# Two heads side by side in the array: scores and values of one attention, rotary scores of another

## The reference

```python
# first block: 8 heads of 64; with 256 tokens each query sees its own block only, causally
q = _rope(_rms_norm(q, q_norm_g[l]), pos)
k = _rope(_rms_norm(k, k_norm_g[l]), pos)
s_own = jnp.einsum('hqd,hjd->hqj', q_c, k_own, ...) * scale
s_own = jnp.where((k_pos[None, :] <= q_pos[:, None])[None], s_own, -jnp.inf)
p = jax.nn.softmax(scores, axis=-1)          # then p @ v, by head

# second block: 6 heads, keys of 128 (own) + 64 (rotary, shared by all heads), values of 128
q = jnp.concatenate([q_nope, q_rope], axis=-1)
k = jnp.concatenate([k_nope, k_rope], axis=-1)      # 256 tokens and 256 of the context: 512 keys
s = jnp.einsum('bqhd,bkhd->bhqk', q_blk, k, ...) * scale
pr = jax.nn.softmax(s, axis=-1)
return jnp.einsum('bhqk,bkhd->bqhd', pr, v)
```

## Time and profile before

| what | value |
|---|---|
| median of 3 runs | 1614.91 us (1614.48 to 1618.3) |
| the profiled execution, its own time | 1612.96 us |
| its span, first to last instruction | 1611.1 us |
| TensorE busy | 1546.0 us (96%) |
| VectorE busy | 407.1 us (25%) |
| ScalarE busy | 301.7 us (19%) |
| DMA, mean | 319 GB/s; from about 685 us on some 428 GB/s in nearly all slices |
| mean granted TensorE clock | 0.996 |

### The profile page before, as it was taken

The page is one execution under the profiler, slowest core; times in us unless marked ns, Lnnn a source line. Parts: engine busy times, 40 slices in busy tenths (PEclk is TensorE's granted clock), DMA queues, the critical chain, the costliest instruction groups (busy, mean ns, idle before and its releaser), DMA issues.

```text
span 1611.1 us, 18676 instructions
## 1 busy us (share of the span) xinstructions
PE 1546.0 (96%) x7234; PEld 851.3 (53%) x7234; DVE 407.1 (25%) x865; ACT 301.7 (19%) x618; POOL 9.1 (1%) x19
## 2 busy tenths in 40 slices
PE   9999999999999999999999999899999999998997
PEld 8666767888888756533333333324433333332332
DVE  1564244222223224431212121111112121111112
ACT  2223131111112234310111011111101110110111
POOL 0000000000000000000000000000000000000000
PEclk9999999999999999999999999999999999999999
DMA  9623675744443120699999999999989999999996
GB/s 389 247 105 128 283 320 190 280 157 157 150 144 123 53 105 24 280 428 428 423 428 428 429 429 428 429 428 427 418 362 426 430 429 428 428 429 428 428 428 272
DMA packets 44897, 513.34 MB, mean 319 GB/s; under 512 B 5120, under 2 KB 5264, under 8 KB 7088
## 3 DMA queue, kind: packets, MB, share of 16 engines
q1 hardware_dynamic: 43632, 507.69, 76.2%
q0 software_dynamic: 1216, 4.96, 0.9%
HBM read 511.58 MB, written 1.06 MB: 318 GB/s over the span
## 4 chain that ended last, share of the span: by engine, by line
PE 74%; DMA 20%; DVE 3%; ACT 2%; issue 1%; DVEq 0%; ACTq 0%; SPq 0%
PE bank L1165 26%; PE bank L615 12%; DMA ring<-in_gate_w 9%; PE bank L864 9%; DMA ring<-in_up_w 8%; PE bank L873 5%; DMA ring<-in_down_w 3%; PE bank L1257 3%; PE bank L1137 2%; PE bank L1197 2%; PE bank L1032 2%; PE bank L724 2%; PE bank L1182 1%; PE bank L653 1%; PE bank L680 1%; DVE squares L1865 1%
## 5 line engine op out<-in xcount | busy, mean ns | idle before, releaser
L1165 PE MATMUL bank<-ring,probs_slab 128*64 128x512 f32 x2928 | 660.6, 598 | 33.3 <-DMA ring<-in_gate_w 12.7
L1165 PEld LDWEIGHTS bank<-ring,probs_slab 128*64 128x64 f32 x2928 | 200.7, 137 | 424.4 <-issue 380.8
L864 PE MATMUL bank<-normed,ring 128*128 128x256 f32 x704 | 153.7, 379 | 0.0
L864 PEld LDWEIGHTS bank<-normed,ring 128*128 128x128 f32 x704 | 133.7, 190 | 19.0 <-issue 0.8
L2210 DVE TENSOR_TENSOR normed<-bank,big_slab 128x512 f32<-128x512 f32 x31 | 21.4, 692 | 430.7 <-PE bank L1182 430.7
L615 PE MATMUL bank<-normed,ring 128*128 128x256 f32 x448 | 98.5, 380 | 0.8 <-ACT normed L1393 0.8
L615 PEld LDWEIGHTS bank<-normed,ring 128*128 128x128 f32 x448 | 84.2, 190 | 15.1 <-issue 2.8
L2000 DVE SCALAR_TENSOR_TENSOR big_slab<-bank,par,big_slab 128x255 f32<-128x255 f32 x88 | 42.4, 482 | 166.3 <-ACT big_slab L1527 158.7
L873 PE MATMUL bank<-big_slab,ring 128*128 128x256 f32 x352 | 77.6, 379 | 0.0
L873 PEld LDWEIGHTS bank<-big_slab,ring 128*128 128x128 f32 x352 | 66.9, 190 | 9.1
L1197 PE MATMUL bank<-squares,mixed_slab 64*128 64x512 f32 x248 | 61.6, 615 | 6.3 <-ACT squares L1678 6.3
(11 more groups left out here) (332 smaller groups left out, 1179.7 us busy)
## 6 DMA issues: line engine op xcount, KB each, us to landing
ring<-in_up_w SPq DMA_DIRECT2D x63, 2048.0 KB, 22.1
ring<-in_down_w SPq DMA_DIRECT2D x63, 2048.0 KB, 22.2
ring<-in_gate_w SPq DMA_DIRECT2D x62, 2048.0 KB, 22.1
ring<-in_front_w SPq DMA_DIRECT2D x97, 1024.0 KB, 6.3
ring<-in_down_w SPq DMA_DIRECT2D x2, 1024.0 KB, 25.1
residual<-in_x SPq DMA_DIRECT2D x4, 256.0 KB, 6.5
memory_slab<-in_mem SPq DMA_DIRECT2D x1, 1024.0 KB, 16.4
context_slab<-in_ctx POOLq DMA_DIRECT2D x1, 1024.0 KB, 9.4
```

Of the source, the lines that this page charges most:

```text
L864: mm = pe.matmul(bank[bank_at][:, half * T:(half + 1) * T], w[:, (half * DC + k) * P:(half * DC + k + 1) * P], H[:, k, :], start=(k == 0), ...
L1165: mm = pe.matmul(to[half * SLOTS:(half + 1) * SLOTS, :], tokens(k), weights[:, i * D + half * HALF:i * D + (half + 1) * HALF], start=(k == ...
```

## The change

The scores of two heads are issued together in both attentions, and the products of two heads that use different halves of the array are written alternately. In the first attention `scores(j)` opens the banks of both heads before the first product; `attend(j)` alternates the two heads. In the second attention the rotary product of a head uses only the 64 rows on which its queries lie (K = 64), against rotary keys that are simply there twice, so the copy and the two fills go. Heads are handled in pairs there: the scores of two heads for the same t in one call, and the order on TensorE, VectorE and ScalarE is by pair and t instead of by head.

```diff
-            def scores(h):
...
-                a = HEAD * (h % 2)
-                q, k = QK[a:a + HEAD, h // 2, :], QK[a:a + HEAD, 4 + h // 2, :]
-                pe.matmul(o[:, 0:P], q[:, 0:P], k[:, 0:P], start=True, stop=True)
-                end(pe.matmul(o[:, P:P + T], q[:, P:T], k, start=True, stop=True))
+                to = [begin(f"s{2 * j + i}") for i in range(2)]
+                q, k = [[QK[HEAD * i:HEAD * (i + 1), at, :] for i in range(2)] for at in (j, 4 + j)]
+                for i in range(2):
+                    pe.matmul(to[i][:, 0:P], q[i][:, 0:P], k[i][:, 0:P], start=True, stop=True)
+                for i in range(2):
+                    end(pe.matmul(to[i][:, P:P + T], q[i][:, P:T], k[i], start=True, stop=True))
...
+                for tokens, keys, at, first, last in ((0, 0, 0, True, True), (P, 0, P, True, False),
+                                                      (P, 1, T, False, True)):
+                    for i in range(2):
+                        h = 2 * j + i
+                        mm = pe.matmul(o[HEAD * i:HEAD * (i + 1), tokens:tokens + P],
+                                       V1[:, keys, h * HEAD:(h + 1) * HEAD], PTu[:, h % 4, at:at + P],
+                                       start=first, stop=last)
...
             def latent_scores(h, t):
-                o = begin(f"a{h}{t}")
-                pe.matmul(o[:, :], QN[:, h, t * P:(t + 1) * P], KN[:, h, :], start=True, stop=False)
-                end(pe.matmul(o[:, :], QR[:, h // 2, t * P:(t + 1) * P], KR_of[h % 2],
-                              start=False, stop=True))
+                at = slice(t * P, (t + 1) * P)
+                to = [begin(f"a{h + i}{t}") for i in range(2)]
+                for i in range(2):
+                    pe.matmul(to[i][:, :], QN[:, h + i, at], KN[:, h + i, :], start=True, stop=False)
+                for i in range(2):
+                    of = slice(ROPE * i, ROPE * (i + 1))
+                    end(pe.matmul(to[i][:, :], QR[of, h // 2, at], KR[of, :], start=False, stop=True))
...
-            for h in range(LHEADS):
-                if h + 1 < LHEADS:
-                    latent_scores(h + 1, 0)
-                    latent_scores(h + 1, 1)
+            for h in range(0, LHEADS, 2):
                 for t in range(2):
...
+                    for i in range(2):
+                        pe.wait_ge(s_soft, HEADS + XHEADS + 2 * h + 2 * t + i + 1)
+                        o = begin(f"at{h + i}{t}")
...
+                    if h + 2 < LHEADS:
+                        latent_scores(h + 2, t)
+                latent_attend(h)
+                if h + 2 < LHEADS:
+                    latent_attend(h + 1)
...
-            step(dve.tensor_copy(KR_of[0][0:ROPE, :], KR[0:ROPE, :]))
-            step(dve.memset(KR_of[0][ROPE:P, :], 0.0))
-            step(dve.memset(KR[0:ROPE, :], 0.0))
...
-            latent_softmax(0, "max")
-            for h in range(LHEADS):
-                latent_softmax(h, "normalise")
-                if h + 1 < LHEADS:
-                    latent_softmax(h + 1, "max")
+            latent_max(0, 0)
+            latent_max(0, 1)
+            for h in range(0, LHEADS, 2):
                 for t in range(2):
...
+                    for i in range(2):
+                        read(dve, f"a{h + i}{t}")
+                        normalise(((0, 2 * T),), HEADS + XHEADS + 2 * h + 2 * t + i, 2 * t + i)
+                    if h + 2 < LHEADS:
+                        latent_max(h + 2, t)
```

More of the change, by code:

```diff
@@ L82 @@
     + ["qp0", "qp1", "qn0", "qt0", "qt1", "qn1", "qn2"]
[L83 to L86, removed]
+    + ["a00", "a10", "a01", "a11"]
+    + [n for h in range(0, LHEADS, 2) for n in
+       [name for t in range(2) for name in
+        [f"at{h}{t}", f"at{h + 1}{t}"]
+        + ([f"a{h + 2}{t}", f"a{h + 3}{t}"] if h + 2 < LHEADS else [])]
+       + [f"ao{h}"] + ([f"ao{h + 1}"] if h + 2 < LHEADS else [])]
     + ["xt0", "xt1", "xt2", "xt3", f"ao{LHEADS - 1}"]
@@ L212, in build_program @@
         QR = KX[:, 4:7, :]
-        KR_of = [UF.rearrange("p t n -> p (t n)"), KR]
         QN = CT[:, 0:6, :]
@@ L726, in cross_values, with scores @@
                 end(mm)
[L729 to L730 removed]
+            def scores(j):
+                if j == 0:
                     pe.wait_ge(s_rot, 4)
[L732 to L736 removed]
+                to = [begin(f"s{2 * j + i}") for i in range(2)]
[4 more added lines that the diff above has]
+                    end(pe.matmul(to[i][:, P:P + T], q[i][:, P:T], k[i], start=True, stop=True))
             def turn_probs(h):
@@ L749, in attend @@
                 read(pe, f"t{2 * j}")
[L750 to L758, removed]
+                for tokens, keys, at, first, last in ((0, 0, 0, True, True), (P, 0, P, True, False),
[5 more added lines that the diff above has]
+                                       start=first, stop=last)
                 end(mm)
-            for h in range(4):
-                scores(h)
+            for j in range(2):
+                scores(j)
             cross_values(0, 0)
@@ L767, in _ @@
                 turn_probs(h)
-            for h in range(4, 8):
-                scores(h)
+            for j in range(2, 4):
+                scores(j)
             cross_values(1, 0)
@@ L1002, in _ @@
             latent_scores(0, 1)
-            for h in range(LHEADS):
-                if h + 1 < LHEADS:
-                    latent_scores(h + 1, 0)
-                    latent_scores(h + 1, 1)
+            for h in range(0, LHEADS, 2):
                 for t in range(2):
[L1008 to L1015, removed]
+                    for i in range(2):
+                        pe.wait_ge(s_soft, HEADS + XHEADS + 2 * h + 2 * t + i + 1)
+                        o = begin(f"at{h + i}{t}")
+                        for c in range(4):
+                            mm = pe.transpose(o[:, c * P:(c + 1) * P],
+                                              PR[:, 2 * t + i, c * P:(c + 1) * P], ident)
+                        end(mm)
+                    if h + 2 < LHEADS:
[3 more added lines that the diff above has]
+                    latent_attend(h + 1)
             for j in range(4):
@@ L1579, in _, with latent_exps @@
                 copy_out(f"qn{j}", QN[:, 2 * j:2 * j + 2, :], pair(slot_bank(f"qn{j}")))
-            def latent_exps(h):
-                for t in range(2):
[L1583 to L1588, removed]
-            for h in range(LHEADS):
-                if h + 1 < LHEADS:
[L1591 to L1598, removed]
+            def latent_exps(h, t):
+                for i in range(2):
+                    unit = HEADS + XHEADS + 2 * h + 2 * t + i
+                    exps(((0, 2 * T),), unit, 2 * t + i, slot_bank(f"a{h + i}{t}"),
+                         (NOPE + ROPE) ** -0.5, done=f"a{h + i}{t}")
+            load_table(ACT.Exp)
+            latent_exps(0, 0)
+            latent_exps(0, 1)
+            for h in range(0, LHEADS, 2):
+                for t in range(2):
+                    for i in range(2):
+                        name = f"at{h + i}{t}"
+                        copy_out(name, PT[:, 4 * i:4 * i + 4, t * P:(t + 1) * P],
+                                 slot_bank(name).rearrange("p (c n) -> p c n", c=4))
+                    if h + 2 < LHEADS:
+                        latent_exps(h + 2, t)
+                for i in range(2):
+                    copy_out(f"ao{h + i}", MIX[:, h + i, :], slot_bank(f"ao{h + i}")[:, 0:T])
             load_table(ACT.Sqrt)
@@ L2072, in _, with latent_max @@
             turn("qt1", QR[:, 2:3, :], SQ[:, 5:6, :], cos2, sin2, 1)
-            def latent_softmax(h, part):
-                for t in range(2):
[L2076 to L2081, removed]
-            latent_softmax(0, "max")
-            for h in range(LHEADS):
-                latent_softmax(h, "normalise")
-                if h + 1 < LHEADS:
-                    latent_softmax(h + 1, "max")
+            def latent_max(h, t):
+                for i in range(2):
+                    raw_max(((0, 2 * T),), HEADS + XHEADS + 2 * h + 2 * t + i, f"a{h + i}{t}",
+                            (NOPE + ROPE) ** -0.5)
+            latent_max(0, 0)
+            latent_max(0, 1)
+            for h in range(0, LHEADS, 2):
+                for t in range(2):
+                    for i in range(2):
+                        read(dve, f"a{h + i}{t}")
+                        normalise(((0, 2 * T),), HEADS + XHEADS + 2 * h + 2 * t + i, 2 * t + i)
+                    if h + 2 < LHEADS:
+                        latent_max(h + 2, t)
             for j in range(4):
```

1 line of the change is left out of this document (removed).

## The result

| kernel | median, us | lowest to highest | ratio to before, 95% interval |
|---|---|---|---|
| before | 1614.63 (13 runs) | 1614.01 to 1618.3 | |
| changed | 1625.98 (13 runs) | 1620.81 to 1629.35 | 1.0063 [1.0054, 1.0072] |

Slower by 0.6%. The profiled execution of the changed kernel took 1629.35 us, the longest of its 13 runs, and its span is 1627.5 us: what its profile shows is the slow end of what this kernel does. Where kernels of different sections are compared, the ratio to the kernel before, run beside each of them, is the surer measure; medians of the kernel before differ by up to 1 us between series (1614.63 here, 1615.59 in another).

What follows compares the result with a forecast made beforehand. TensorE was taken to bound the stages touched. Second attention +6.8, first attention -0.4 and clock +1.7 gave +8.1 us on the profiled 1612.96; with the median 1.95 above, 1623.0, forecast as 1622, range 1616 to 1629.

Steps and rivals of the forecast that it cites:

- First attention, -0.4: First attention: 0.4 us saved, bounds -0.8 to +0.3, mostly from alternating value products; its score products already overlapped.
- What the 64 rows save, 5.15 less 1.8: Second attention: six overlapping rotary pairs save 5.15 us; switching between 128 and 64 rows costs 1.8, bounds 0 to 2.7.
- Three waits of 3.0: Second attention: TensorE idles 3.0 us three times before transposes, waiting for VectorE's normalisation; 9.0 us, plus 0.7 at the end.
- +6.8: Second attention in sum, before any clock loss: 6.8 us longer, from saving, switching, waits, cold starts and late copies.
- The clock, +1.7: Second attention: half-clock stretches after the new waits cost 1.7 us, one fall less a little; bounds 0 and 5.7.
- the bound of 5.7: Second attention: upper bound of the clock loss in us, if the clock falls at each wait.
- rival 1: Second attention: waits come as worked out, with no, one or two clock falls; 1622 us, 1618 to 1626; chance 0.66.
- rival 2: Second attention: clock falls at every wait, costing 5.7 us instead of 1.7; 1626, up to 1631; chance 0.11.
- The price of a fall: Second attention: 6.85 us at half clock, 3.0 of it waiting, costs 1.9 us; stretch length from the earlier trace's one fall.
- Nothing swallowed by the experts: Experts: weight transfers and TensorE shift together with the attention's end, so the delay reaches the kernel's end.
- rival 4: Experts: their DMA hides most of the delay, leaving under 4 us; 1614.5 to 1618; chance 0.12.
- Rivals 3 and 5: Second attention: rotary products don't overlap, 1624.6 us, chance 0.05; or waits at most 1.2 us each, faster, chance 0.06.

## Why the prediction was right or wrong

The direction and the range were right: 1622 forecast, 1625.98 measured, slower. The mechanism was right too, order and waits; the clock was taken too small. Step by step:

- **First attention, -0.4.** 0.3 in both profiles that have the change. Right, and the reason too: the heads overlapped before.
- **What the 64 rows save, 5.15 less 1.8.** The saving is there (two rotary products in the time of one). Switching costs 0.4 us a pair, 0.2 each way: 6 x 0.4 = 2.4. In the changed kernel the waits swallow three of the ways out, which leaves 1.8, the forecast's term. Its split, 0.11 in and 0.3 out, was not what the runs show; the errors cancel, and that part is luck.
- **Three waits of 3.0.** 2.67, 2.94 and 2.67 us idle by the page, 2.83 from the end of the scores to the transposes at the first; 0.69 at the tail, where 0.7 stood. Right in place and cause, and in length to 0.2 us; the products in the waits confirm the sum of the stage at full clock, +7.0 where +6.8 was forecast.
- **The clock, +1.7.** This is the term that was mis-sized. I took "one fall less a little"; the profile has three falls in the stage, which cost 5.4 us there, near the bound of 5.7. By all runs, with and without products in the waits, it is 4.9 us by the medians and 3.2 by the ratios. With it the sum is 6.8 - 0.4 + 3.2 to 4.9 = 9.6 to 11.3; measured are 10.2 by the ratio and 11.35 by the medians.
- **Which rival it was.** The time lies in the range of rival 1, 1618 to 1626, by 0.02 us. The profile, with its three falls, shows the mechanism of rival 2, which had 0.11. The profiled run is the longest; eleven of the other twelve had a higher granted clock and so presumably fewer falls, and what share of the 13 belongs to either rival is not known.
- **The price of a fall.** The forecast took it from the one fall of the trace before, which came with 32-row products behind a wait of 0.86 us. The kernel with eight banks and 128 rows has the same products behind the same wait at 694.87, and its granted clock stays at 1.00 from 694 to 706. So such a stretch does not bring a fall each time, and it was no measure of how many falls three waits would bring.
- **Nothing swallowed by the experts.** 977 us after the stage in both. Right, so rival 4 falls.
- **Rivals 3 and 5** fall: the rotary products overlap, and the waits are 2.7 us and more.

Settled by runs are the parts of the order and of the 64 rows, and that filling the waits gives time back; the size of the clock's part is known to some 2 us. That the falls in the stage follow from the waits is read from where they lie. The six profiles without an open wait before transposes (before, the first attention alone, the 64 rows head by head, and the three with eight banks) have none in the stage, nor has the one with products in the waits; of the three with such waits the changed kernel has three falls and the other two one each, behind the opening's wait. Why three waits bring three falls in one profile and one in another, where each is 1.8 us long instead of 2.7 to 2.9, is open. The single runs fit: the changed kernel took 1621.09 and 1623.13 us in the two with a mean granted clock of 0.997, and 1627.04 and 1629.35 in the two with 0.991. That the varying number of falls makes its wide spread of 8.5 us is likely by these, but was not tried by itself.

## What to carry to other kernels

When products are grouped so that two results come out together, count again what stood between a result and its first use: the saving on TensorE (here 0.47 us a pair) is small against a softmax's round trip over three engines (2.8 us). With four banks the order by pairs could not keep the old distance (1.9 us of waiting for a bank were left); with eight it did. An idle stretch of TensorE is charged twice where the clock falls behind it: here 3 to 5 us on top of 8.3. Before pairing products by hand, look whether their starts already coincide in the timeline.

## What the runs showed of the hardware

- With waits of 2.7 to 2.9 us and transposes behind them the granted clock fell to 1.2 GHz for 3.4 to 6.8 us at a time, 13.7 us in all in one stage; with products of 128x128 in the same waits it stayed at 2.4 GHz (1.00 over the stage). With three waits of 1.8 us it fell once, for 3.4 us.
- The same 32-row products behind a wait of 0.86 us stood at 1.2 GHz for 6.8 us in one profile and at 2.4 GHz throughout in another.
- Products on opposite halves of the rows overlap even where one head's two products stand wholly ahead of the other's in the program: the first records of heads 0 and 1 start at 110.245 and 110.258 us before the change. TensorE does not start its products strictly in the order written.
- A change from 128 to 64 rows costs 0.2 us, and the way back 0.2 us (1.05 us from start to start instead of 0.86), in a stage that is otherwise dense.
